# Time mixing: the gate projection's slices stand behind 6 of a body's 18 stages, twice as many at each

## What is computed

```python
def trunk_layer(x, past, lp):
    h = rmsnorm(x, lp['norm1_g'])
    P = h @ lp['w_in']
    P_rw, P_sa, P_ret, P_gate = split_cols(P, (RW_COLS, SA_COLS, RET_COLS, GATE_COLS))
    y_rw, s_rw_new, shift_new = rwkv_mixer(P_rw, shift_rw, s_rw, lp)
    ...
    gates = jax.nn.sigmoid(P_gate.astype(F32)).astype(x.dtype).reshape(B, L, N_BRANCH, D_MODEL)
    merged = (gates[:, :, 0] * (y_rw @ lp['w_br_rwkv']) + ...)

def rwkv_scan(r, decay, k, v, kk, a, S0):
    def step(S, inp):
        removed = jnp.einsum('bhvk,bhk->bhv', S, kk_t)
        S = (S * w_t[:, :, None, :] - removed[..., None] * (kk_t * a_t)[:, :, None, :]
             + v_t[..., None] * k_t[:, :, None, :])
        return S, jnp.einsum('bhvk,bhk->bhv', S, r_t)
```

## Time and profile before

| what | value |
|---|---|
| median of 3 runs | 2688.83 us (2687.6 to 2692.62) |
| the profiled execution: its time, its span | 2687.32 us, 2685.5 us |
| PE busy, of the span | 2576.5 us, 96% |
| DVE, POOL, ACT busy | 1308.0, 1059.5, 561.7 us |
| mean granted clock of TensorE | 0.981 of full speed |
| bodies 1 to 5 of the first layer | 590.5 to 778 us of the span |
| all six bodies of the second layer | 1877 to 2105.6 us |

### The profile page before, as it was taken

One profiled execution on the slowest core, in us unless ns is written; L12 is line 12 of the kernel. 1 busy time (PEld: TensorE's weight loads), 2 busy tenths in 40 slices (PEclk: granted clock), 3 DMA queues, 4 the chain that ended last, 5 costly groups with the idle time before them and its releaser, 6 DMA issues.

```text
span 2685.5 us, 61384 instructions
## 1 busy us (share of the span) xinstructions
PE 2576.5 (96%) x24742; PEld 2392.1 (89%) x24742; DVE 1308.0 (49%) x2242; ACT 561.7 (21%) x1117; POOL 1059.5 (39%) x596
## 2 busy tenths in 40 slices
PE   7997999999989999999999979999999899999998
PEld 7986887799969999999989868877999799999998
DVE  5357886554545621121544588756444555211215
ACT  2022222411123210010210222223211322110112
POOL 4522333221225555565544223323112255555553
PEclk9998999999999999999999989999999999999999
DMA  5212112311135222222232111122111352222221
GB/s 192 88 40 74 48 56 70 107 56 40 52 121 164 92 80 87 84 81 86 79 131 80 57 50 64 56 74 104 52 40 46 144 162 80 85 81 87 80 84 67
DMA packets 66731, 222.81 MB, mean 83 GB/s; under 512 B 8257, under 2 KB 9025, under 8 KB 65473
## 3 DMA queue, kind: packets, MB, share of 16 engines
q1 hardware_dynamic: 45360, 160.59, 17.7%
q10 hardware_dynamic: 21136, 58.84, 6.3%
HBM read 190.38 MB, written 29.03 MB: 82 GB/s over the span
## 4 chain that ended last, share of the span: by engine, by line
PE 83%; DVE 9%; DVEq 5%; issue 2%; ACT 1%; DMA 0%; ACTq 0%
PE dense L526 67%; PE mix L526 14%; DVEq L1545 5%; DVE region_b L1804 1%; DVE region_b L1905 1%; PE mix L957 1%; DVE region_b L1916 0%; DVE x L1857 0%; ACT region_b L1075 0%; DVE region_b L1581 0%; DVE region_b L1976 0%; PE dense L957 0%; DVE region_b L2010 0%; DVE region_b L1892 0%; DVE x L1809 0%
## 5 line engine op out<-in xcount | busy, mean ns | idle before, releaser
L510 POOL TENSOR_SCALAR w_hi<-w_raw 128x1024 fp32r<-128x1024 f32 x296 | 311.7, 1053 | 1579.1 <-PE dense L526 1229.8
L513 POOL TENSOR_TENSOR w_lo<-w_raw,w_hi 128x1024 fp32r<-128x1024 f32 x296 | 747.7, 2526 | 24.6
L526 PE MATMUL dense<-act_hi,w_hi 128*128 128x288 f32 x2272 | 689.1, 314 | 29.1 <-DVE act_lo L1563 13.6
L526 PE MATMUL dense<-in_hi,w_hi 128*128 128x288 f32 x2432 | 679.3, 294 | 10.3 <-DVE in_lo L2034 8.7
L526 PE MATMUL dense<-in_lo,w_hi 128*128 128x288 f32 x2432 | 678.9, 295 | 0.0
L526 PE MATMUL dense<-act_lo,w_hi 128*128 128x288 f32 x2272 | 651.9, 298 | 0.0
L526 PE MATMUL dense<-act_hi,w_lo 128*128 128x288 f32 x2272 | 535.9, 297 | 0.0
L526 PE MATMUL dense<-in_hi,w_lo 128*128 128x288 f32 x2432 | 522.5, 296 | 0.0
L526 PEld LDWEIGHTS dense<-act_hi,w_hi 128*128 128x128 f32 x2272 | 433.4, 191 | 86.0 <-issue 44.6
L526 PEld LDWEIGHTS dense<-in_hi,w_hi 128*128 128x128 f32 x2432 | 458.9, 189 | 12.4 <-DVE in_lo L2034 8.9
L526 PEld LDWEIGHTS dense<-in_lo,w_hi 128*128 128x128 f32 x2432 | 459.3, 189 | 0.0
(11 more groups left out here) (200 smaller groups left out, 2648.7 us busy)
## 6 DMA issues: line engine op xcount, KB each, us to landing
w_raw<-in_stream SPq DMA_DIRECT2D x296, 512.0 KB, 3.2
y_mix<-gate_scratch ACTq DMA_DIRECT2D x48, 288.0 KB, 2.9
gate_scratch<-region_b ACTq DMA_DIRECT2D x36, 288.0 KB, 2.3
x_scratch<-x ACTq DMA_DIRECT2D x2, 2304.0 KB, 12.3
y_scratch<-y_mix ACTq DMA_DIRECT2D x2, 2304.0 KB, 7.8
x<-x_scratch ACTq DMA_DIRECT2D x2, 2304.0 KB, 9.9
y_mix<-y_scratch ACTq DMA_DIRECT2D x2, 2304.0 KB, 9.7
gate_scratch<-region_a ACTq DMA_DIRECT2D x12, 288.0 KB, 2.1
```

Source lines behind the costliest of these rows:

```text
L510: nc.gpsimd.tensor_scalar(w_hi[:, v, :], w_raw[:, s, :], 1.0, 1.0, ALU.mult, ALU.mult).then_inc(w_high, 1)
L513: nc.gpsimd.tensor_tensor(w_lo[:, v, :], w_raw[:, s, :], w_hi[:, v, :].bitcast(F32), ALU.subtract).then_inc(w_split, 1)
L526: return nc.tensor.matmul(out, lhsT, rhs, start=start, stop=stop, skip_group_check=True)
```

## The change

One line: the weights of bodies 1 to 4. Every body keeps its sum of 36, so the numbers of slices in each body stay as they were, and so do all of the work and its operands. Bodies 0 and 5 and everything outside the bodies are untouched.

```diff
-BODY_SHARE = ((3,) * 12,) + ((0, 3, 0, 3, 0, 3, 3, 0, 3, 0, 3, 0, 3, 3, 3, 3, 3, 3),) * 4 + ((2,) * 3,)
+BODY_SHARE = ((3,) * 12,) + ((0, 6, 0, 0, 0, 6, 0, 0, 6, 0, 0, 0, 6, 0, 6, 0, 6, 0),) * 4 + ((2,) * 3,)
```

## The result

The changed kernel takes 2705.9 us in the median of four runs (2703.6 to 2710.03), the kernel before beside it 2690.7 us (2687.6 to 2692.8): ratio 1.0059, with a 95% interval of 1.0042 to 1.0077. It is slower, by some 15 us between the medians (the interval is 11 to 21 us).

What follows compares the result with a forecast made beforehand. PE's own work was taken to bound the bodies. New waits of 15.1 us a layer less 7.2 saved gave 15.8 us for both layers, plus 12.4 for the clock: 2717 us by the median, range 2700 to 2726.

Steps and rivals of the forecast that it cites:

- The likeliest case: Whole kernel: new waits plus the clock falling in bodies 1 to 3, 2717 us (2708 to 2728), chance 0.47.
- the second case, waits only: Whole kernel: new waits cost time but the clock holds, 2705 us (2700 to 2708), chance 0.37.
- the signs that I had set for being wrong: level_m1's second half not waiting, an unexpected queue holding PE over 2 us, or a different count of clock falls.
- The excursions: Bodies 1 to 4: 24 fewer PE turns to slice groups a layer, about 0.3 us each, 7.2 us saved.
- A: Turn to level_m1(0), bodies 1 to 4: PE waits 1.55 us for ACT's three copies; 5.0 us a layer new.
- B: level_x(n) to level_m1(n+1), stages 6, 13, 15: second half waits 0.41 us for DVE's update; 4.9 us a layer.
- C: level_x(4) to the next gram, stage 17: PE waits 0.88 us in four bodies, 3.5 us a layer.
- D: Body 1, stage 16, slice 84: PE waits 1.7 us a layer for DVE's gate_half, between 0 and 2.3.
- The clock: Bodies 1 to 3 behind turn: four of six thin stretches drop to half clock, 3.1 us each, 12.4 us.
- "Faster": Bodies, levels 1, 3 and 4: saved turns to slices outweigh waits below 7.2 us a layer; 2685 us, chance 0.04.
- more low stretches come: Half clock also ahead of the next gram and in body 4: 2729 to 2742 us, chance 0.06.
- the table does nothing: Whole kernel: waits and saving cancel, nothing measurable, 2684 to 2694 us, chance 0.06.

Runs made afterwards that it cites:

- Experiment 4: Changed kernel with equal weights, one slice behind each of the 18 stages of bodies 1 to 4: 2708.5 us, ratio to the kernel before 1.0074.
- Experiment 3: Changed kernel with body 3's slices spread 3, 3, 4, 4, 3, 2, so its weights' tile ends with stage 14: 2702.3 us, ratio to before 1.0048.
- Experiment 7: Changed kernel with ACT repeating its third copy behind turn twice, a drain behind each, in bodies 0 to 4: 2726.8 us, ratio to before 1.0136.
- experiment 8: Changed kernel with five groups of slices in body 1 and eight groups in bodies 2 to 4: 2680.9 us, ratio to before 0.9974.
- experiment 9: Changed kernel with eight groups of slices in bodies 1 to 4 and DVE's gate_half ahead of rwkv_stage: 2684.6 us, ratio to before 0.9984.
- experiment 5: Changed kernel with five groups of 3 to 5 slices at other places in bodies 1 to 4: 2711.1 us, ratio to before 1.0082.
- experiment 6: Changed kernel with eight groups of slices in bodies 1 to 4, four of them behind levels 3 and 4: 2695.4 us, ratio to before 1.0023.
- experiment 1: Changed kernel with the slices of stage 5 moved to stage 3, ahead of level_m1(0): 2698.8 us, ratio to before 1.0032.

## Why the prediction was right and wrong

The direction and the range were right: 2705.9 us lies between 2700 and 2726, on the slower side that had 0.90. The likeliest case was not the one that came: I put 2717 with the clock falling, and what came is nearest to the second case, waits only, 2705 us. By the signs that I had set for being wrong, two came: an unforeseen queue, POOL's split, held PE for 2.18 us, and the clock's count was one and not four. Step by step:

- **The excursions, 0.30 us each: right.** Experiment 4 shows 0.32 to 0.36 us in a body without other waits.
- **Waits A, B, C, D: right in place and nearly in size.** From start to start A is 1.56 us in bodies 1 to 3 (forecast 1.55) and 0.92 in body 4, where step 4's copies are smaller, which I had not taken into account. B is 0.31 to 0.32 (0.41) in bodies 1 to 3, at the three stages named and not at stage 10; in body 4, whose step is half as large, it is two waits of 0.18, 0.37 us a stage. C is 0.79 and at the last body 0.89 (0.88). D is 1.57 (1.7). A layer has thus 4.4 + 3.9 + 3.3 + 1.6 = 13.2 us of the waits foreseen, where I had 15.1 (A less what was due before, as there).
- **That the sum fits so well (15.8 us, and the medians differ by 15.2) is partly luck.** Experiment 3 shows a term that was not in the sum at all: POOL's split under rwkv_stage of body 3, 1.4 us a layer beyond C (2.18 to 0.78), and 1.6 more where the clock fell behind it. I had looked at POOL's tile only at body 1, where its earlier end helps (D), and had then said that everything else stays covered; in body 3 the tile ends with slice 119, the first of stage 16, and its split falls on DVE. The 1.9 us a layer by which the waits foreseen were too large paid for most of it. In the traces the bodies lost 17.1 us: 2 x (13.2 + 1.4 - 7.2) = 14.8 by these terms, 1.6 by the one low stretch, and 0.7 us remain, of which a gap of 0.4 on "issue" in body 2 of layer 2 is one part.
- **The clock: this step of the likeliest case failed, in count and in price.** I wrote that "four of the six such stretches lose it" and that one costs 3.1 us, 12.4 us in all. None of the eight A waits of the changed kernel lowered the clock. I had reasoned from the row at 246.87 that small matmuls without a gap are enough and carried this from 64\*64 matmuls of 288 columns to the bodies' 64\*64 matmuls of 64; nothing in the bodies bore that out, and body 0, whose wait of 1.2 us kept the clock, was the nearer row. Experiment 7 shows what does it here: the same place, the same matmuls around it, a wait of 2.89 instead of 1.56 us, and the clock falls six times in six. It also gives the price, 1.6 us and not 3.1, as the stretches last 3.4 us here, half of the 6.8 that I took from two other stages. The gap rule of the Trainium skill, "TensorE: Matmul & The Clock Gate", section "Why this matters for your kernels", by which I had put the sum at 15.8 us, chose the right case for wait A; but the clock also fell behind waits of 2.16 to 2.89 us (experiment 7 and the last section), shorter than the gap that it warns of, and there the measurement decides.
- **Rivals.** "Faster" needed waits below 7.2 us a layer; they were 14.6, body 4's gram included. That more low stretches come and that the table does nothing are excluded by the trace and the interval.

Whether fewer excursions can pay was open after the prediction. Experiments 8 and 9 answer it: they do, if the slices stay at the places where a copy is late, and if neither DVE's evacuation of a half nor POOL's split lands on the path.

## What to carry to other kernels

Filler work beside a chain has three prices that must be looked up apart: turning aside (here 0.3 us each time), the waits that it no longer covers, and the moment at which it hands back its buffers. The last decided here four times (D, body 4's gram, experiments 5 and 6): for each group ask which half it opens, where in the other engine's order the evacuation of that buffer stands, and what the end of a tile starts on a third engine. For a claim on the clock take the nearest row with the same matmuls and the same kind of wait, not the most striking one; and when a table is tuned, measure body by body, since the bodies added up (8.6 us foreseen, 7.8 by the bodies of the trace, 6.4 between the medians) where whole kernels misled.

## What was not expected of the hardware

- DVE's operations that only read and write SBUF take far longer while POOL makes the low part: L1630 and L1631, 0.42 and 0.29 us in experiment 3, took 1.26 and 2.43 us in the changed kernel, L1631 2.56 us in experiment 6 (0.42 for its width without POOL). It is not only in the tables that lose by it: L1659 and L1660 of body 3 take 1.37 and 2.84 us in the kernel before too, where PE has other work meanwhile. The Trainium skill, "SBUF — State Buffer", section "SBUF: two separate sides", tells of a port pair that DVE and GpSimd share under an exclusive lock. The trace agrees in that one DVE instruction lasted about as long as L513 (2.43 against 2.39 us in the changed kernel) and the next ones were short again; no run here separates the lock from other causes.
- After waits of 1.56 to 1.85 us in the bodies the clock never fell, over all kernels here. After waits of 2.16 to 2.19 us ahead of body 4's gram it fell in 7 of 10 cases over five kernels, one of the two layers often and the other not, with the same instructions around. At each of 2.36 us and more (experiments 5, 6 and 7, twelve places) it fell, in body 3 of experiment 5 while the wait still ran. What decides in the middle stays open.
- In the bodies PE sometimes stood with "issue" as its releaser, where the profile shows nothing that it waited for: 0.4 us once in the changed kernel, 1.17 in experiment 1, up to 1.85 in experiments 8 and 9 (layer 2, body 4), at other places in each table. In all 16 of these gaps above 0.6 us the instruction queue (q8 in the page) had started a transfer of 16 KB 2.3 to 2.9 us before PE went on, which by chance would be so in about one of nine. It looks as if PE waited there for its own program, but no run tests it. Such a gap costs up to 1.4 us of a body and moves with the table, so it sets a floor to what one body in one trace can show.
